# Mixer 0 of a float32 three-block network: another order of tiles, tap matmuls in one stretch, squares summed on VectorE

## The reference

```python
u = xn @ w_in + b_in                       # 1024 -> 2048 channels, in four quarters
val, gate, gate_in, rec_in = split(u, 4)   # v, g, x, r below, 4 tiles of 128 channels each
y = val * sigmoid(gate)                    # "glu"
y = causal_dwconv(y, conv_w) + conv_b      # 31 taps per channel
ya = silu(layernorm(y, ln_g, ln_b))        # over 512 channels
xr = causal_dwconv(rec_in, lru_w) + lru_b  # 4 taps
r, i = sigmoid(xr @ w_a + b_a), sigmoid(xr @ w_x + b_x)   # heads of 64
a = exp(-8 * softplus(-lam) * r)
h = scan(h * a + sqrt(1 - a * a) * i * xr) # along the sequence
yb = h * gelu(gate_in)
out = concat(ya, yb) @ w_out
```

## Time and profile before

| | us |
|---|---|
| median of three runs | 4849.92 (4848.38 to 4857.04) |
| profiled execution, its own time | 4855.08 |
| its span, first to last instruction | 4853.0 |
| mixer 0: first matmul to first matmul of the output projection | 14.5 to 437.7 |
| TensorE's mean granted clock, share of full | 0.922 |

### The profile page before, as it was taken

How to read it: one execution, slowest core, us unless ns; L and a number is a source line. 1 busy time by engine, 2 the same in 40 slices (tenths; PEclk the granted TensorE clock), 3 DMA queues, 4 the chain that set the end, 5 groups by cost and what they waited for, 6 DMA issues and landing times.

```text
span 4853.0 us, 49440 instructions
## 1 busy us (share of the span) xinstructions
PE 4352.4 (90%) x20306; PEld 3431.6 (71%) x20306; DVE 1906.3 (39%) x2426; ACT 1236.2 (25%) x1576; POOL 1049.4 (22%) x508
## 2 busy tenths in 40 slices
PE   7797799999859999988999996898999999999778
PEld 5556688888736666667888875787788877866656
DVE  1854312222262222313222225521566666356552
ACT  3234321111222222332111113222222222144411
POOL 1101322222321111232222224122111111022143
PEclk9898899999968998989999997999999999899888
DMA  2001011111110000111111111223111112132142
GB/s 81 26 18 61 26 48 48 48 48 50 42 47 18 18 18 14 31 70 36 52 49 48 48 48 62 83 91 119 66 47 41 60 55 104 33 114 64 59 156 87
DMA packets 76841, 270.97 MB, mean 56 GB/s; under 512 B 8772, under 2 KB 9416, under 8 KB 72648
## 3 DMA queue, kind: packets, MB, share of 16 engines
q1 hardware_dynamic: 76616, 267.82, 16.6%
HBM read 219.55 MB, written 48.23 MB: 55 GB/s over the span
## 4 chain that ended last, share of the span: by engine, by line
PE 76%; DVE 15%; ACT 4%; POOL 2%; DMA 2%; issue 1%; SPq 0%; DVEq 0%; POOLq 0%; ACTq 0%
PE ps L349 48%; PE ps L378 6%; PE ps L720 2%; PE ps L2052 2%; PE ps L1383 2%; DVE t L488 2%; PE ps L2064 2%; PE ps L1367 2%; PE ps L2060 1%; PE ps L1385 1%; PE ps L3102 1%; DVE ca L785 1%; PE ps L2105 1%; DMA gb<-g_keep 1%; DVE n L3119 1%
## 5 line engine op out<-in xcount | busy, mean ns | idle before, releaser
L295 POOL TENSOR_TENSOR wlo<-wraw,whi 128x1024 fp32r<-128x1024 f32 x301 | 723.0, 2402 | 2890.2 <-ACT whi L287 2882.2
L349 PE MATMUL ps<-xhi,whi 128*128 128x512 f32 x3024 | 1000.7, 413 | 161.8 <-DVE xlo L510 89.2
L349 PE MATMUL ps<-xlo,whi 128*128 128x512 f32 x3024 | 958.8, 399 | 0.0
L349 PE MATMUL ps<-xhi,wlo 128*128 128x512 f32 x3024 | 956.3, 398 | 0.0
L287 ACT ACTIVATE whi<-wraw 128x1024 fp32r<-128x1024 f32 x301 | 318.9, 1060 | 2115.4 <-PE ps L349 1796.9
L349 PEld LDWEIGHTS ps<-xhi,whi 128*128 128x128 f32 x3024 | 569.7, 194 | 308.1 <-DVE xlo L510 86.3
L349 PEld LDWEIGHTS ps<-xlo,whi 128*128 128x128 f32 x3024 | 585.1, 193 | 127.3
L349 PEld LDWEIGHTS ps<-xhi,wlo 128*128 128x128 f32 x3024 | 584.0, 193 | 126.6
L545 DVE TENSOR_TENSOR ps<-ps,t 128x1024 f32<-128x1024 f32 x161 | 198.5, 1233 | 1178.2 <-PE ps L349 1177.1
L378 PE MATMUL ps<-xhalf,whi 128*128 128x512 f32 x1024 | 380.4, 454 | 6.3 <-POOL wlo L295 6.3
L349 PE MATMUL ps<-xhalf,whi 128*128 128x512 f32 x1024 | 286.1, 403 | 33.1 <-DVE xhalf L510 21.2
(11 more groups left out here) (488 smaller groups left out, 5184.6 us busy)
## 6 DMA issues: line engine op xcount, KB each, us to landing
wraw<-in_w_dram SPq DMA_DIRECT2D x301, 512.0 KB, 3.5
g_keep<-gates SPq DMA_DIRECT2D x64, 256.0 KB, 2.4
gb<-g_keep SPq DMA_DIRECT2D x32, 512.0 KB, 5.6
p_keep<-stage SPq DMA_DIRECT2D x30, 512.0 KB, 2.9
x<-in_x_dram SPq DMA_DIRECT2D x8, 1024.0 KB, 9.8
x_keep<-x SPq DMA_DIRECT2D x8, 1024.0 KB, 3.8
x<-x_keep SPq DMA_DIRECT2D x4, 1024.0 KB, 7.8
n<-p_keep SPq DMA_DIRECT2D x8, 512.0 KB, 6.8
```

The lines of the kernel that those rows point to most:

```text
L295: ge.own().tensor_tensor(K.lo(c), K.raw[:, c % NRAW, :], K.hi(c).bitcast(F32), SUB).then_inc(*K.G(("lo", c)))
L349: done = mm(into[a][:, h, :], wt, x[h], start=(i == 0 and j == 0), stop=(i == n - 1 and j == 2), skip_group_check=True)
```

## The change

The tile order puts both VectorE convolutions' tiles first, then the tiles of one TensorE convolution, then the other's around two r tiles. The four background queues get their rates step by step: (1.8, 2.2, 1.2, 0) while TensorE has taps to do, (0.5, 0, 0.45, 0) when it has none and the norm has not begun, and (1, 0, 1, 0.8) afterwards. The squares of the entry and of the layer norm are added up in one tile by VectorE, and TensorE sums that tile once; in the entry this follows all eight blocks. Lambda is copied and its exponential is taken at the start of mixer 0, and the rest of the rates is made at the start of the first recurrence.

```diff
@@ line 400 of the kernel before
-def columns_tensor(pe, K, n, i, sq, last):
-
-    b = take(pe, K, K.Q, n, "sum", hold=True) if i == 0 else K.bank_of[(n, "sum")]
-    pe.wait_ge(*K.at(n, "sq", i))
+def columns_tensor(pe, K, n, acc):
+
+    b = take(pe, K, K.Q, n, "sum")
+    pe.wait_ge(*K.at(n, "add"))
     for k in range(8):
-        d = pe.e.matmul(K.ps[:, b, k:k + 1], sq[:, part(k)], K.ones[:, 0:1], start=(i == 0 and k == 0), stop=(i == last and k == 7), skip_group_check=True)
-    d.then_inc(*K.T((n, "summed", i), (n, "sum")))
-    if i == last:
-        K.Q.give((n, "sum"))
+        d = pe.e.matmul(K.ps[:, b, k:k + 1], acc[:, part(k)], K.ones[:, 0:1], start=(k == 0), stop=(k == 7), skip_group_check=True)
+    d.then_inc(*K.T((n, "sum")))
@@ line 472 of the kernel before
             se.own().activation(hi, x, ACT.Copy, scale=N.gain(i)).then_inc(*K.S((n, "high", i)))
-        if N.after is None:
-            if i >= 2:
-                se.wait_ge(*K.at(n, "summed", i - 2))
-            se.own().activation(N.sq[i % 2], X[:, i, :], ACT.Square).then_inc(*K.S((n, "sq", i)))
-        elif i == 0:
+        if i == 0:
             se.own().activation(N.acc[:, :], X[:, i, :], ACT.Square).then_inc(*K.S((n, "sq", 0)))
@@ line 510 of the kernel before
             ve.own().scalar_tensor_tensor(out=lo, in0=x, scalar=N.gain(i), in1=hi.bitcast(F32), op0=MUL, op1=SUB).then_inc(*K.V((n, "low", i)))
+        if Y is None and i > 0:
+            enter_add(ve, K, N, i)
@@ line 559 of the kernel before
-    for i in range(7):
-        next(product)
-        columns_tensor(pe, K, N.name, i, N.sq[i % 2], 7)
-    columns_tensor(pe, K, N.name, 7, N.sq[1], 7)
-    m = next(product)
+    m = None
+    while m is None:
+        m = next(product)
+    columns_tensor(pe, K, N.name, N.acc)
     stat_back_tensor(pe, K, N.name, N.sq[0])
@@ line 577 of the kernel before
-TILES0 = ["v1", "g1", "v0", "g0", "r0", "v2", "g2", "v3", "g3", "r1", "r2", "r3", "x0", "x1", "x2", "x3"]
+TILES0 = ["v0", "g0", "r0", "v2", "g2", "r1", "v1", "g1", "v3", "g3", "r2", "r3", "x0", "x1", "x2", "x3"]
 BY_PE = (1, 3)
@@ line 586 of the kernel before
-    def __init__(self, rate):
-        self.rate, self.due, self.jobs = rate, 0.0, deque()
-
-    def step(self):
-        self.due += self.rate
+    def __init__(self):
+        self.due, self.jobs = 0.0, deque()
+
+    def step(self, rate):
+        self.due += rate
         while self.due >= 1:
@@ line 619 of the kernel before
         self.diag = K.sb([128, NDIAG, 128], ctx=c, name="diag")
-        self.wide, self.sq = N.acc, (N.s0, N.s1)
+        self.acc, self.sq = N.acc, (N.s0, N.s1)
@@ line 652 of the kernel before
-    on_v, on_p, on_l, on_c = (Background(r) for r in (1.2, 1.25, 1.0, 0.8))
+    on_v, on_p, on_l, on_c = (Background() for _ in range(4))
     done, norm = set(), deque(["norm"])
@@ line 674 of the kernel before
                 on_l.jobs.append(job("lru", j))
-        for b in (on_v, on_p, on_l, on_c):
-            b.step()
+        rates = (1.8, 2.2, 1.2, 0.0) if on_p.jobs else (0.5, 0.0, 0.45, 0.0) if norm else (1.0, 0.0, 1.0, 0.8)
+        for b, rate in zip((on_v, on_p, on_l, on_c), rates):
+            b.step(rate)
         norm_begins()
@@ line 748 of the kernel before
                 d.then_inc(*K.T(("mu", h)))
+            yield from wait_steps(5)
+            K.Q.give(("mu", 0))
+            K.Q.give(("mu", 1))
+            yield
+            columns_tensor(pe, K, "conf", M.acc)
             yield from wait_steps(3)
-            for i in range(4):
-                columns_tensor(pe, K, "conf", i, M.sq[i % 2], 3)
-                if i == 2:
-                    K.Q.give(("mu", 0))
-                    K.Q.give(("mu", 1))
-                yield
-            yield from wait_steps(2)
-            stat_back_tensor(pe, K, "conf", M.wide)
+            stat_back_tensor(pe, K, "conf", M.sq[1])
             yield
@@ line 771 of the kernel before
+    ve.own().tensor_copy(M.sp[:, :], K.span("lru_lambda")).then_inc(*V(("lambda",)))
+
     def rates():
-        ve.own().tensor_copy(M.sp[:, :], K.span("lru_lambda")).then_inc(*V(("lambda",)))
         for _ in softplus_vector(ve, K, "lambda", M.sp[:, :], [M.spt[:, i, :] for i in range(4)]):
             pass
         ve.own().tensor_scalar(M.sp[:, :], M.sp[:, :], 8.0, None, MUL).then_inc(*V())
         ve.own().tensor_scalar(M.neg[:, :], M.sp[:, :], -1.0, None, MUL).then_inc(*V(("rates",)))
+
+    def norm_add(i):
+        ve.wait_ge(*K.at("conf", "sq", i))
+        ve.own().tensor_tensor(M.acc[:, :], M.acc[:, :], M.sq[i % 2][:, :], ADD).then_inc(*V(("conf", "add"), ("conf", "add", i)))
@@ line 791 of the kernel before
             RI = M.RI[:, j % 2, :]
+            if j == 0:
+                rates()
             ve.wait_ge(*K.at("ri", j))
@@ line 821 of the kernel before
                     ve.own().scalar_tensor_tensor(out=x, in0=K.bank("mu", h), scalar=-1.0 / 512, in1=x, op0=MUL, op1=ADD).then_inc(*V(("centred", i), ("free", ("mu", h))))
+                if i >= 2:
+                    norm_add(i - 1)
                 yield
-            yield from wait_steps(3)
+            norm_add(3)
+            yield
+            yield
             stat_mean_vector(ve, K, "conf", 512)
             yield
-            stat_wide_vector(ve, K, "conf", M.wide[:, :])
+            stat_wide_vector(ve, K, "conf", M.sq[1][:, :])
             yield from wait_steps(2)
@@ line 843 of the kernel before
-    def settle():
-        settle_vector(ve, K, N)
-        rates()
-
-    mixer0_drive(K, first_tiles(walk(ve, K, nothing, 8, 16, 2), settle), evac, jobs)
+    mixer0_drive(K, first_tiles(walk(ve, K, nothing, 8, 16, 2), lambda: settle_vector(ve, K, N)), evac, jobs)
     YS = M.YS
@@ line 859 of the kernel before
     se.wait_ge(*K.at("constants"))
+    se.wait_ge(*K.at("lambda"))
+    softplus_scalar(se, K, "lambda", M.sp[:, :], M.spt[:, 0, :])
@@ line 899 of the kernel before
                 se.wait_ge(*K.at("centred", i))
-                if i >= 2:
-                    se.wait_ge(*K.at("conf", "summed", i - 2))
-                se.own().activation(M.sq[i % 2][:, :], M.CA[:, i, :], ACT.Square).then_inc(*S(("conf", "sq", i)))
+                if i == 3:
+                    se.wait_ge(*K.at("conf", "add", 1))
+                dst = M.sq[i % 2] if i else M.acc
+                se.own().activation(dst[:, :], M.CA[:, i, :], ACT.Square).then_inc(*S(("conf", "sq", i)))
                 yield
@@ line 927 of the kernel before
-    def settle():
-        settle_scalar(se, K, N)
-        se.wait_ge(*K.at("lambda"))
-        softplus_scalar(se, K, "lambda", M.sp[:, :], M.spt[:, 0, :])
-
-    mixer0_drive(K, first_tiles(walk(se, K, weights_scalar, 8, 16, 2), settle), evac, jobs)
+    mixer0_drive(K, first_tiles(walk(se, K, weights_scalar, 8, 16, 2), lambda: settle_scalar(se, K, N)), evac, jobs)
     YS = M.YS
```

## The result

The changed kernel took 4808.0 us (median of 4 runs, 4806.24 to 4814.13) against 4853.48 of the kernel before in the same comparison: ratio 0.9905, 95% interval 0.9883 to 0.9927. Run again later it gave 0.9894 (0.9876 to 0.9912). Forecast: 4804. The saving is 45.5 us in these medians, with 35 to 57 us inside the interval, against a forecast of 46.4 by the profile. The profiled executions say where: mixer 0 hands over to the output projection at 388.03 us, forecast 391.3, before 437.68. The rest of the kernel took 4416.8 us after it and 4415.3 before.

The account below looks back on a forecast made before the run. TensorE, busy 90% of the span, was taken as the bound, so gains come from its idle time, low clock or removed matmuls. Entry 18.2 plus middle 28.2 gave -46.4 us: 4808.7 profiled, 4804 as median; range 4784 to 4824.

Parts of the forecast that it names:

- The entry: Start of mixer 0: one set of column sums, rates moved away; first scaling at 46.3 instead of 64.47 us, -18.2.
- Rival C: Entry adds on VectorE cost 3.43 us each, not 1.23; entry gives 9 us less, total 4813; chance 0.05.
- the uncovered chain: Entry statistics from end of columns to reciprocal root, with TensorE now waiting: 5.4 us, 40.8 to 46.2.
- Steps 2 to 49: Driver steps, one per weight block, without TensorE taps: waits 7.7 at r0's gate product, 12.6 after g1; low clock 1.8, 2.0.
- Step 50: Weight block where conv 1's taps start: r1's gate product behind one tap, 4.1 us wait, 1.8 low clock.
- Tap phase: Taps beside v3, g3, r2, r3: TensorE work 151 us, 2.7 wait at conv 3's first tap, about 1 clock; ends at 312.
- Rival D: Taps beside weight blocks run at the low clock; all 31 steps lose 148 us, giving 4952; chance 0.03.
- Steps 82 to 113: Tiles x0 to x3 to the output projection, 79.3 us; waits 7.0 gate product, 3.7 columns, 2.2 transposes, 5.2 end.
- the middle: Mixer 0 from TensorE's restart to the output projection: -28.2 us, 5 of matmuls, 23 of idle and low clock.
- A: VectorE later than counted in steps 11 to 50 or around x0: about +20 us, 4824; chance 0.15.
- E: Entry's 18 us given back at weight block 50, middle gains nothing: 4850; chance 0.02.
- B: Waits after g1 and in x0 overlap better: some low clock and half the waits vanish, 21 us less, 4783; chance 0.08.

Follow-up runs that it names:

- e8: Changed kernel with the entry's seven adds on POOL instead of VectorE; ratio to before 0.9886, mixer 0 ends at 390.97 us.
- e11: The changed kernel itself, unedited, run once more; ratio to before 0.9894, mixer 0 ends at 388.20 us.
- e3: Changed kernel with the old entry: column sums per block, rates ahead of the first scaling; ratio to before 0.9878, mixer 0 ends at 399.49 us.
- e5: Changed kernel with the recurrence's rates made right behind the entry's last add, not at the first recurrence; ratio to before 0.9873, mixer 0 ends at 381.86 us.

## Why the prediction was right, step by step

*The entry*, -18.2: measured 64.47 to 45.83 at the first scaling (-18.6) and 66.91 to 48.26 at the restart. Blocks 24.2 us for 24.6, columns end 40.5 for 40.8, the uncovered chain 5.3 for 5.4, adds 1.22 to 1.23 each, add 7 done at 33.6 for 32.7. Rival C is out for this entry, and e8 shows what POOL's work beside it would have cost.

*Steps 2 to 49*: the last convolution instruction of r0 ended at 84.5 (84.8), TensorE waited 7.82 (7.7), low clock 1.5 (1.8). g1's scaling stood at 139.49 (139.9), the first tap waited 12.55 (12.6) and took 3.78 for 1.72 (2.0 more forecast). The match of the low clock is luck: in e11, the same kernel, the product took 6.72 us after the same wait, so 3.1 of low clock. The waits are the part with most hand work behind it, and they held within half a microsecond, because VectorE executes a list whose order the code fixes and its durations repeat from profile to profile. The sum was right by the rates, and their own price was hidden in it: e3 and e5 say 6 to 8 us, more than their 4.5, because after the shorter wait the clock stayed at 1.00 and the collision with POOL's split fell on another instruction.

*Step 50*: here I was wrong in a detail. I set the gate product of r1 at step 50, behind one tap, with 4.1 us of wait and 1.8 of low clock. The trace has it one step later, after a block and two more taps, at 152.77, with no wait:

```profile
143.15 3.78 PE ps L716 x4
146.93 2.40 PE ps L349 x6
149.33 3.44 PE ps L716 x8
152.77 3.62 PE ps L734 x8
```

VectorE's convolution was done at 151.02, as forecast (151.5), but TensorE asked for it only after that. I had given the recurrence's job on TensorE one pause too few when I counted. 5.9 us of the sum (4.1 and 1.8) were not there.

*Tap phase*: from 156.4 to the end of the last tap at 307.7, with a wait of 2.90 us at conv 3's first tap (forecast 2.7, and about 1 of clock). End of step 81: 307.7 for 312, 4.3 early: 0.4 brought along and 5.9 of the miscount, less 2.0 that I had set too small, 1.0 of low clock at the block behind conv 1's first tap (2.40 us for 1.39) and 1.0 of wait and clock at conv 3's. Rival D is out: clock 0.99. What I said against it was too wide, though: before the change TensorE made the layer norm's column sums at a granted clock of 0.63 while it was busy 18.3 of 20 us, and in the part from 372 to 380 us, where it never stood still, at 0.50.

```profile
360.00:380.00 20.00, 18.30 (x76) 15.52 (x76) 14.75 (x9) 5.51 (x5) 0.00 (x0) 0.63 0.01 3
```

*Steps 82 to 113*: 80.3 us for 79.3. Waits 5.84 at the gate product (7.0), 5.44 at the columns (3.7), 1.08 at the transposes (2.2), 5.23 at the end (5.2). The causes are those forecast: VectorE stood 9.79 us for ScalarE's square 2 behind the gates of the last recurrence. One term was left out: the low clock behind the 5.44 us wait. The column sums there, priced at 1.7 us, took 3.56 at a granted clock of 0.50.

```profile
343.88 2.55 DVE L776 TENSOR_TENSOR t<-t 128x1024 f32<-128x1024 f32 x2 [9.79 <-ACT t L906]
346.58 3.54 PE L406 MATMUL ps<-const,t 128*128 128x1 f32 x16 [5.44 <-DVE t L776]
```

*The sum*: -49.7 at 388.03 against -46.4; the 3.3 are the miscounted wait (5.9) less small losses. The entry gave 18.7 us (18.2 forecast) and the middle 31.0 (28.2): 20.1 of idle time and 10.9 of busy time, matmuls that are gone and low clock together. The kernel won 45.5 us in the medians and 48.2 in the profiled spans, so the rest of the kernel took 1.5 us more in these two executions. Against the saving of 46.4 that is 0.9 off by the medians; the 4 us between 4804 and 4808.0 are mostly the kernel before, whose median is 4849.92 of the three executions shown and 4853.48 of four. With an interval 21 us wide, so close a match of the whole time is chance, and only the stages inside mixer 0 test the working. Rivals A and E did not happen, nor B as a mechanism: the waits at the first tap and the first gate product were not half but whole; only the one that I had added by miscount was missing. In e8 a POOL add and a VectorE low part together took 3.2 us, where their own durations sum to 3.66. The Trainium skill ("SBUF — State Buffer", the shared port pair) says that such a pair, a VectorE instruction with two SBUF inputs and a GpSimd one that reads SBUF, keep each other out for the whole instruction. The rows agree on which engines hold each other up, but show a little less than the whole.

## What to carry to other kernels

In a kernel where each engine runs a fixed list, count what stands ahead of the instruction that another engine waits for, and by its place in the list, not by the busy share: VectorE was 40% busy over the span and 10 us late at the one scaling that mattered. Moving work to a phase where its engine waits (here ten taps by a rate of 0.3 in place of 0.5, and 22 small instructions into a gap) gave 16 us more for two short edits, while the same idea in the last phase lost, because there the moved work was itself the last chain. Change the rates with the order: the new order and entry with the old rates kept 3 of 50 us, and the entry alone was worth 12.

## What was not expected of the hardware

A wait of 2.1 us left TensorE's clock high for the next product (3.67 us for eight instructions, in e3 and e5), while one of 2.62 us before the change was followed by 5.42 for the same work, and 7.82 by 5.13 or 6.72. The length of the wait alone does not settle it: after the same 2.90 us of standing, conv 3's first tap took 1.96 us in e3 and 3.65 in e5, for 1.72 at the full clock. What decides between the two was not tried apart. A VectorE instruction on 4 columns can be held up as one on 1024 (2.35 us beside POOL's split); in the changed kernel 22 of the 23 stand at the first recurrence and ran in 4.4 us with none held up.
